# Gates and the next layer's shifts and scales: from two-column matmuls on TensorE to multiply-and-sum over weight rows on VectorE

## The reference: what is computed

```
mod_l = c2 @ w_mod[l] + b_mod[l]              # (2, 3072): shift, scale, gate; 1024 each
h     = x * (1 + scale) + shift
proj  = h @ w_in[l]                           # Hyena, differential attention, MLA, paths, merge gates
...   three branches, each times its SiLU path, through w_branch, gated by sigmoids, summed
out   = merged @ w_out[l]
x     = LayerNorm(alpha * x + gate * out)
```

## Time and profile before

| | us |
|---|---|
| median of 3 runs (2127.22 to 2134.22) | 2133.4 |
| profiled execution, its own time | 2133.02 |
| its span in the trace | 2130.8 |
| PE busy | 1995.7 (94%) |
| DVE busy | 1035.8 (49%) |
| ACT busy | 638.4 (30%) |
| POOL busy | 518.6 (24%) |
| mean granted TensorE clock | 0.966 of full |

### The profile page before, as it was taken

The page is one execution under the profiler, slowest core; times in us unless marked ns, Lnnn a source line. Parts: engine busy times, 40 slices in busy tenths (PEclk is TensorE's granted clock), DMA queues, the critical chain, the costliest instruction groups (busy, mean ns, idle before and its releaser), DMA issues.

```text
span 2130.8 us, 29090 instructions
## 1 busy us (share of the span) xinstructions
PE 1995.7 (94%) x12004; PEld 1722.8 (81%) x12004; DVE 1035.8 (49%) x1486; ACT 638.4 (30%) x1107; POOL 518.6 (24%) x248
## 2 busy tenths in 40 slices
PE   6799989999999999999989999899999999999995
PEld 4578689877886888899886786898778777789995
DVE  3548587355443444322256786845452444442425
ACT  2221322344323343321233122123342344432221
POOL 0211124221231110244222121331222311114640
PEclk9899999999999999999989999999999999999997
DMA  8001012211211211232431110221112111112331
GB/s 325 30 30 40 30 50 80 60 50 40 96 59 50 73 55 58 77 124 85 157 121 40 30 41 30 70 66 54 45 46 105 44 33 41 50 48 99 107 118 50
DMA packets 49818, 149.52 MB, mean 70 GB/s; under 512 B 11030, under 2 KB 12566, under 8 KB 48664
## 3 DMA queue, kind: packets, MB, share of 16 engines
q1 hardware_dynamic: 49688, 147.67, 21.1%
HBM read 141.07 MB, written 6.59 MB: 69 GB/s over the span
## 4 chain that ended last, share of the span: by engine, by line
PE 76%; DVE 13%; ACT 4%; issue 3%; POOL 2%; DMA 1%; SPq 1%; DVEq 0%; ACTq 0%; POOLq 0%
PE PS L691 16%; PE PS L696 16%; PE PS L692 16%; PE PS L727 5%; PE PS L869 3%; PE PS L744 3%; PE PS L715 2%; PE PS L986 2%; PE PS L778 2%; PE PS L765 2%; PE PS L762 2%; PE PS L920 2%; ACT work L1039 1%; DVE work L1670 1%; ACT Wh L1039 1%
## 5 line engine op out<-in xcount | busy, mean ns | idle before, releaser
L1621 POOL TENSOR_TENSOR Wl<-W,Wh 128x1024 fp32r<-128x1024 f32 x196 | 439.4, 2244 | 1406.7 <-ACT Wh L1039 1363.4
L691 PE MATMUL PS<-Hh,Wh 128*128 128x320 f32 x2112 | 638.7, 317 | 15.0 <-ACT work L1163 5.0
L692 PE MATMUL PS<-Hl,Wh 128*128 128x320 f32 x2112 | 626.8, 311 | 0.0
L691 PEld LDWEIGHTS PS<-Hh,Wh 128*128 128x128 f32 x2112 | 401.2, 190 | 41.0 <-issue 25.1
L692 PEld LDWEIGHTS PS<-Hl,Wh 128*128 128x128 f32 x2112 | 401.3, 190 | 2.5 <-issue 1.2
L696 PE MATMUL PS<-Hh,Wl 128*128 128x320 f32 x2112 | 331.4, 309 | 0.9 <-POOL Wl L1621 0.9
L696 PEld LDWEIGHTS PS<-Hh,Wl 128*128 128x128 f32 x2112 | 315.1, 188 | 1.5 <-POOL Wl L1621 1.5
L1039 ACT ACTIVATE work<-PS 128x640 f32<-128x640 f32 (+8 forms) x298 | 176.9, 602 | 355.3 <-PE PS L727 97.8
L1275 DVE TENSOR_REDUCE st<-PS 128x1 f32<-128x640 f32 (+1 forms) x160 | 114.8, 718 | 181.1 <-PE PS L920 91.8
L1039 ACT ACTIVATE Wh<-W 128x1024 fp32r<-128x1024 f32 x196 | 185.8, 950 | 56.2 <-DMA W<-in_w_out 28.3
L1138 ACT ACTIVATE th<-PS 128x640 f32<-128x640 f32 x64 | 45.1, 705 | 343.0 <-PE PS L696 343.0
(11 more groups left out here) (178 smaller groups left out, 2600.4 us busy)
## 6 DMA issues: line engine op xcount, KB each, us to landing
W<-in_w_in SPq DMA_DIRECT2D x132, 512.0 KB, 3.5
W<-in_w_mod SPq DMA_DIRECT2D x32, 512.0 KB, 3.6
W<-in_w_branch SPq DMA_DIRECT2D x48, 256.0 KB, 2.6
pmod_w<-in_w_mod SPq DMA_DIRECT2D x8, 1024.0 KB, 17.4
W<-in_w_out SPq DMA_DIRECT2D x16, 512.0 KB, 3.6
work<-in_x_sample SPq DMA_DIRECT2D x2, 2048.0 KB
x_mid<-work SPq DMA_DIRECT2D x1, 2560.0 KB, 8.5
work<-x_mid SPq DMA_DIRECT2D x1, 2560.0 KB
```

The lines of the kernel that those rows point to most:

```text
L691: pe.matmul(out, Wh[:, b, kk, :], xh[:, kk, t], start=kk == 0, stop=False)
L692: pe.matmul(out, Wh[:, b, kk, :], xl[:, kk, t], start=False, stop=False)
L1621: return pool.tensor_tensor(out, in_, high.bitcast(f32), ALU.subtract)
```

## The change

The 32 blocks are formed without TensorE. The host lays w_mod out by rows: for each block a 128 x 1024 tile whose partition p holds all 1024 weights of output p. Both conditioning rows are put through SiLU as two rows of 1024, stored to memory, and loaded back as `cb`, repeated on all 128 partitions, once per layer (`cload`). A block is then two VectorE `tensor_tensor_reduce` instructions, one per conditioning vector: weights times `cb`, summed over 1024 elements, with the bias as start value and the result in one column of `modc`. A new step `mload` has ScalarE issue the load of a weight tile, and wait first for the VectorE step that last read that buffer. There are three such buffers for the first 17 blocks of layer 0 and one for all others.

The steps leave latent attention and the place after LayerNorm: they now stand among the path tiles, after the merge pairs, and (layer 0 only) behind the wo steps. gmod and nmod no longer take a PSUM slot, nor a place among the `W` tiles. SyncE waits for the 17th block of layer 0 before it loads layer 1's tables. Some tables move to other addresses, and one more constant is loaded at the start.

```
-def weave(a, b): ...
+MOD_PATH, MOD_MERGE, MOD_OUT = ((0, 1, 1, 1), (0, 0, 1, 1)), ((2, 2, 1, 2, 2, 1, 2, 2), (1,) * 6 + (0, 0)), ((1,) * 7 + (0,), (0,) * 8)
+MODS = [[("gmod", g) for g in range(KD)] + [("nmod", g) for g in range(2 * KD if l < DEPTH - 1 else 0)] for l in range(DEPTH)]
+def mod_buffer(l, m):
+    return m % 3 if l == 0 and m < EARLY[0] else 0
+class ModSteps:
+    def loads(self):
+        while self.loaded < len(MODS[self.l]):
+            at, users = mod_user(self.l, self.loaded)
+            if at and users[at - 1][0] == self.l and users[at - 1][1] >= self.done:
+                break
+            steps.append(("mload", self.loaded))
+            self.loaded += 1
+    def take(self, n):
+        for _ in range(n):
+            steps.append(MODS[self.l][self.done])
+            self.done += 1
+            steps += self.loads()
...
-    s += head(0, 2) + head(0, NT - 1) + attention_steps("ml", MH, weave(merge_steps(1), gmods[:KD - 2] + nmods[:NMOD_EARLY - 2]), head)
-    s += path_steps(2) + merge_steps(2) + gmods[KD - 2:] + nmods[NMOD_EARLY - 2:NMOD_EARLY]
+    s += head(0, 2) + head(0, NT - 1) + attention_steps("ml", MH, merge_steps(1), head)
+    for c, step in enumerate(path_steps(2)):
+        s += [step] + ([("cload", 0)] + mods.loads() if c == 0 else []) + mods.take(MOD_PATH[l][c])
+    for d in range(KD):
+        s += merge_steps(2)[2 * d:2 * d + 2] + mods.take(MOD_MERGE[l][d])
     for d in range(KD):
         s += [("wo", d)]
         if d:
             s += [("xt", d - 1)]
+        s += mods.take(MOD_OUT[l][d])
...
-    return s + [("xt", KD - 1), ("ln", 0)] + nmods[NMOD_EARLY:]
+    return s + [("xt", KD - 1), ("ln", 0)]
...
+                        sp.wait_ge(*mod_done(l, EARLY[l] - 1))
                         layer_tables(l + 1)
...
-                    if kind in ("nmod", "gmod"):
-                        ...
-                        for k in range(KD):
-                            last = pe.matmul(ps[:, 0:2], W[:, g % NW, k, :], ccol[:, k, :], ...)
...
+                    if kind == "cload":
+                        act.wait_ge(c_saved, 16)
+                        act.dma_start(cb..., c_silus....partition_broadcast(128)).then_inc(c_here, 16)
+                    elif kind == "mload":
+                        at_, users = mod_user(l, i)
+                        if at_:
+                            act.wait_ge(*mod_done(*users[at_ - 1]))
+                        act.dma_start(modw[mod_buffer(l, i)], A["w_mod_rows"][len(MODS[0]) * l + i])\
+                           .then_inc(mod_here[mod_buffer(l, i)], 16)
...
+                    elif kind in ("gmod", "nmod"):
+                        dve.wait_ge(mod_here[mod_buffer(l, n)], 16 * (mod_user(l, n)[0] + 1))
+                        for j in range(2):
+                            ins = dve.tensor_tensor_reduce(mod_early if n < EARLY[l] else mod_late, modw[mod_buffer(l, n)],
+                                                           cb[:, j], scale, bmods[:, at_, m:m + 1], ALU.mult, ALU.add,
+                                                           modcs[:, at_ % 2, m, j:j + 1])
+                            if j == 0:
+                                link(ins)
+                        ins.then_inc(sems[name], 1)
+                        dve.wait_ge(*mod_done(l, n))
```

More of the change, by code:

```diff
@@ L87, in merge_steps, with mod_user, __init__ @@
     return [(kind, KD * n + d) for d in range(KD) for kind in ("mgate", "mbranch")]
[L90 to L98, removed]
+MOD_PATH, MOD_MERGE, MOD_OUT = ((0, 1, 1, 1), (0, 0, 1, 1)), ((2, 2, 1, 2, 2, 1, 2, 2), (1,) * 6 + (0, 0)), ((1,) * 7 + (0,), (0,) * 8)
+MODS = [[("gmod", g) for g in range(KD)] + [("nmod", g) for g in range(2 * KD if l < DEPTH - 1 else 0)] for l in range(DEPTH)]
+EARLY = [sum(MOD_PATH[l]) + sum(MOD_MERGE[l]) for l in range(DEPTH)]
+assert all(EARLY[l] + sum(MOD_OUT[l]) == len(MODS[l]) for l in range(DEPTH))
+def mod_buffer(l, m):
+    return m % 3 if l == 0 and m < EARLY[0] else 0
+def mod_user(l, m):
+    users = [(a, n) for a in range(DEPTH) for n in range(len(MODS[a])) if mod_buffer(a, n) == mod_buffer(l, m)]
+    return users.index((l, m)), users
+class ModSteps:
+    def __init__(self, l):
+        self.l, self.done, self.loaded = l, 0, 0
+    def loads(self):
+        steps = []
+        while self.loaded < len(MODS[self.l]):
[4 more added lines that the diff above has]
+            self.loaded += 1
+        return steps
+    def take(self, n):
+        steps = []
+        for _ in range(n):
+            steps.append(MODS[self.l][self.done])
+            self.done += 1
+            steps += self.loads()
+        return steps
 def layer_steps(l):
@@ L177 @@
 NP = 5
-SPLIT = [(kind, i) for kind, i in STEPS[0] if owned(kind, i) and kind not in ("nmod", "gmod")]
+SPLIT = [(kind, i) for kind, i in STEPS[0] if owned(kind, i)]
 NSPLIT = len(SPLIT)
@@ L264, in upto_table @@
     for l in range(DEPTH):
-        places = [n for n, step in enumerate(STEPS[l]) if step in SPLIT_AT]
+        steps = [(n, step) for n, step in enumerate(STEPS[l]) if step[0] not in ("gmod", "nmod", "cload", "mload")]
+        places = [n for n, (_, step) in enumerate(steps) if step in SPLIT_AT]
         table[l, STEPS[l].index(("ht", 0))] = 1
         for n, (a, b) in enumerate(zip(places, places[1:])):
-            table[l, a if b - a <= 2 else a + 1] = n + 2
+            table[l, steps[a if b - a <= 2 else a + 1][0]] = n + 2
     return table
@@ L474, in build @@
         rT = raw
+        crow, csg = area(BR, 1024, D)[0:2], th[:].rearrange("p a b -> p (a b)")[0:2, 0:D]
+        cb = area(work, 18432, 2, D)
+        modw = [area(work, off, D) for off in (17408, 5120, 6144)]
+        mod_early, mod_late = raw[:].rearrange("p a b -> p (a b)")[:, 0:D], area(BR, 1024, D)
         PS = [ctx.enter_context(nc.psum_tensor(f"PS{i}", [128, 1024], f32)) for i in range(SLOTS)]
@@ L489, in build @@
         x_saved = sem("x_saved")
+        c_rows = sem("c_rows_ready")
+        c_saved = sem("c_rows_saved")
+        c_here = sem("c_rows_here")
+        mod_here = [sem(f"modulation_weights_here{i}") for i in range(3)]
         consts_here = sem("consts_here")
```

81 lines of the change are left out of this document (44 added, 37 removed).

## The result

The change makes the kernel slower: the median of 9 runs is 2140.74 us (2136.24 to 2145.85), against 2133.4 us for 9 runs of the kernel before on the same chip (2126.89 to 2135.64). The ratio is 1.0042, its 95% interval 1.0027 to 1.0057. The forecast was 2146 us, so the direction was right and the size was 5 us too large. The profiled execution took 2142.03 us with a span of 2139.9 us, against 2133.02 and 2130.8 us: 9.1 us more.

A forecast was written before the change was run, and what follows sets the result against it. TensorE, busy 94% of the span, was taken as the bound on average, with VectorE time free. From 2133.0 us, 27.2 removed and 40.5 added gave 2146.3, so 2146 us; range 2119 to 2172.

The forecast's parts named there:

- The main mechanism: Paths and third merges: ScalarE's wait for VectorE delays Wh copies; 6.7 and 4.0 us at paths, 14.0 and 9.9 at merges.
- rival 4: Loads from ScalarE's queue come late where layer 1 has one buffer, giving about 2155 us; chance 0.04.
- The price of a block: On VectorE: 1.23 us product plus 0.16 us for the sum, 1.39 us an instruction, 2.8 us a block.
- Rival 2: The accumulating VectorE instruction runs at half rate, 5.2 us a block, giving 2210 us; chance 0.10.
- Attention: the step that failed: Latent attention: removing 22 steps at 1.14 us each saves 25.1 us; bounds 38.5 and some 15 us.
- rival 1: Attention gives all 38.5 us back and waits at the blocks are short, 31 us added, giving 2124 us; chance 0.29.
- rival 3: Ten pauses of 2 to 3 us lower TensorE's clock, 2.1 us each, giving 2166 us; chance 0.10.
- The four steps behind layer 0's third merge: Their removal gains nothing by itself, since tile wo 2's late load, behind layer 1's tables, sets the end.
- wo 2 and the low clock behind its pause: Layer 0's output projection: wo 2 starts 2.0 us later and low clock loses 2.1 us, together 4.1 us.
- The delay of wo 6 behind its block: Layer 0's output projection: two more blocks on VectorE put the copy of wo 6 1.4 us later (0 to 3).
- Layer 1 starts 2.1 us sooner behind the norm: After layer 0's LayerNorm: removing four modulation steps that end 2.1 us after VectorE finishes the norm gains 2.1 us.
- The start: One more constant in SyncE's queue ahead of all loads adds 0.45 us.

The follow-up runs named there:

- experiment 1: Changed kernel with each mload among path and third-merge tiles placed behind the next path or mgate tile's copy: 2112.09 us, ratio 0.9904.
- experiment 5: Changed kernel with mloads in the third merge placed behind the next mbranch tile, among paths behind the next path tile: 2101.19 us, ratio 0.9863.
- experiment 2: Changed kernel with each sum over only the first 512 of 1024 products, steps and loads unmoved: 2109.44 us, ratio 0.9892.
- experiment 8: Kernel before the change, with layer 1's merge tiles in attention at layer 0's places, its six modulation steps kept: 2129.95 us, ratio 0.9994.
- experiment 3: Changed kernel with layer 1's merge tiles in attention at their old uneven places, no modulation steps between: 2152.11 us, ratio 1.0095.
- experiment 7: Kernel before the change, with tile wo 2 loaded ahead of layer 1's tables: 2130.18 us, ratio 0.9999.
- experiment 9: Changed kernel with mloads behind the next mbranch tile, plus layer 0's wo 2 and wo 3 loaded ahead of layer 1's tables: 2095.97 us, ratio 0.9831.
- experiment 6: Changed kernel with later mloads, wo 2 loaded ahead of the tables, and two blocks behind each of layer 0's first seven pairs: 2103.39 us, ratio 0.9872.
- experiment 4: Changed kernel with layer 0's tile wo 2 loaded before the wait for block 17 and layer 1's tables: 2131.82 us, ratio 1.0004.

## Why the prediction was right, and where it was wrong

The main mechanism held, in its place and its size: ScalarE's wait for VectorE, taken for the load, delays a copy that TensorE needs. Forecast and measured pauses (us):

| place | forecast | measured |
|---|---|---|
| paths, layer 0 | 1.9, 2.6, 2.2 | 1.69, 1.97, 1.61 |
| paths, layer 1 | 4.0 for two | 1.69, 1.60 |
| double blocks, layer 0 | 3.2, four times | 3.13, 3.13, 3.13, 3.15 |
| lone blocks, layer 0 | 0.4, three times | 0.47, 0.49, 0.47 |
| merge, layer 1 | 0.4 three times, 2.9 three times | 0.47, 1.82, 0.47, 2.84, 2.85, none |

Together 34.6 us forecast, 19.2 + 11.7 = 30.9 measured. The paths cost less than I had (5.3 and 3.3 us for 6.7 and 4.0), and two more places differ. The last block of layer 1 lets no load go, so it holds nothing up; I had counted it. And the 1.82 is rival 4, at one place: the block itself waited for its tile.

```profile
1976.22 1.28 DVE L1374 CUSTOM_DVE_ANT_0 raw<-work,b_mod 128x1024 f32<-128x1024 f32 x1 [2.78 <-DMA work<-in_w_mod_rows]
```

Taking the wait out of the copy's way (experiments 1 and 5) and shortening it (2) both gave most of that back. So this is shown, not argued.

**The price of a block.** Estimated 1.39 us an instruction. All 64 of the trace:

```profile
L1374 DVE DVE_READ_ACCUMULATOR2_ANT modc<- x64: 76/82/85, 888.6 to 2033.5; 128x1 f32 x64
L1374 DVE CUSTOM_DVE_ANT_0 raw<-work,b_mod x50: 1283/1285/2699, 885.9 to 2032.3; 128x1024 f32<-128x1024 f32 x50
L1374 DVE CUSTOM_DVE_ANT_0 BR<-work,b_mod x14: 1283/1285/3294, 1018.9 to 1093.4; 128x1024 f32<-128x1024 f32 x14
```

(minimum, median, maximum in ns, then the first and last start). 1.285 + 0.08 = 1.37 us. The page of the Trainium skill that the prediction weighed, "Vector Engine (DVE) Microarchitecture Reference", section "Points that are easy to get wrong", would have it at half throughput; the measurement decides against it, since a plain product of the same size takes 1.23 us. Rival 2 is out.

**Attention: the step that failed.** I read 1.14 us a step off two layers that differ by ten steps, and gave all 22 that price: -25.1 us. Measured: -25.3 and -12.3, so -37.6 in all, close to my upper bound of 38.5 and to rival 1's first half. Busy time fell by 28.0 us for 16 steps (1.75 each, as counted) and by 11.2 for 6 (1.9 each). The error was in the waits: I took it that TensorE stands still the more, the fewer steps are left, so that 0.61 us of each step's 1.75 comes back. Of 39.2 us of busy time 1.6 came back. TensorE stands still for 4.8 us with 16 steps, for 8.6 with 6 steps or 10.6 with 6 at even places (experiment 8), and for only 7.8 us with none, but for 13.8 with none at the old places (experiment 3). A straight line through two points, between which the places of the merge tiles had changed too, said nothing of the third. Why waits shrink from 6 steps to none at even places is open.

The other half of what I missed is the clock. With the steps in attention its granted clock is below full: 0.98 in layer 0 in all three traces of that order (before, experiments 7 and 8), and 0.97, 0.97 and 0.99 in layer 1. With the steps gone it is 1.00 or 0.99 in layer 0 in all eight traces, and so it is in layer 1 but for experiment 3 (0.98). So part of the 1.75 us is most likely not the step's own work but a lower clock over it and the matmuls around it. The same stretch of layer 0 in experiments 5 and 9, without and with 3.4 us at 1.2 GHz, gives a price:

```profile
658.00:868.50 210.50, 202.67 (x1194) 161.96 (x1192) 96.12 (x176) 89.64 (x182) 29.14 (x16) 1.00 0.11 34
```

```profile
652.90:864.80 211.90, 204.12 (x1194) 162.57 (x1192) 96.08 (x176) 89.61 (x182) 29.14 (x16) 0.99 0.10 34
```

That is 1.4 us. An estimate from it: in the two attention stages TensorE was at 1.2 GHz for 10.2 and 13.7 us before, and for 0 and 3.4 us after, so 20.5 us less, some 8 of the 37.6 us. I had left this term at nothing.

**The clock in paths and merge: left at nothing too.** That is rival 3 in part. The same matmuls were busy 8.4 us longer in layer 0 and 3.4 us longer in layer 1, 11.8 us over 17 pauses (the rival had 20 for ten). Three windows of the kernel after:

```profile
925.00:940.00 15.00, 12.24 (x69) 11.97 (x67) 8.71 (x11) 0.47 (x2) 3.93 (x2) 0.84 0.35 111
940.00:955.00 15.00, 14.16 (x85) 13.89 (x86) 6.13 (x7) 4.03 (x6) 6.91 (x5) 0.89 0.40 123
955.00:985.00 30.00, 23.72 (x150) 23.20 (x149) 17.45 (x22) 4.34 (x6) 11.04 (x7) 0.94 0.38 125
```

Behind the pause that ends at 940.37 TensorE is at 1.2 GHz up to 943.4 and does 11 matmuls in 3.3 us; from 943.5 on it is at 2.4 GHz and does 75 in 11.5 us:

```profile
940.10:943.40 3.30, 3.03 (x11) 3.03 (x12) 0.00 (x0) 1.76 (x3) 2.75 (x2) 0.50 0.68 191
943.50:955.00 11.50, 11.03 (x75) 10.76 (x75) 6.13 (x7) 2.17 (x3) 4.06 (x4) 1.00 0.32 103
```

With layer 0's pauses down to 1.7 us and less (experiment 1) its clock is 1.00, and it is 1.00 with sums of half length (experiment 2) too. So in layer 0 it is shown that the clock is lost with the long pauses and comes back without them. In layer 1 it is less clear: 0.99 in the changed kernel with pauses of up to 2.85 us, 0.96 with nearly the same pauses in experiment 3, still 0.99 in experiments 1 and 2 with pauses of up to 2.07 and 1.78 us, and 1.00 only in experiments 5, 6 and 9, where one pause of 0.73 us is left. The stretches at 1.2 GHz don't answer to the pauses one to one, and what a single pause costs isn't shown.

**The steps without a change.** The four steps behind layer 0's third merge I held to be worth nothing, since a transfer sets wo 2: right, wo 2 starts 32.1 us behind the merge, where I had about 33. The two-column steps were shadowed by that load, and experiments 4 and 7 show the load as the bound and 6.7 us as their price without it. For wo 2 and the low clock behind its pause I had 4.1 us: wo 2 is 1.5 us later, and wo 3 follows it at 9.8 us where it was 7.6, 3.7 together. The delay of wo 6 behind its block was 1.3 us (10.7 against 9.4), forecast 1.4. Layer 1 starts 2.1 us sooner behind the norm, as said: its first tile comes 30.6 us behind wo 7 instead of 32.7.

The start is 3.4 us longer, where I had 0.45. Nearly all of that is chance. In the kernel after, TensorE is at 1.2 GHz from 414.4 to 417.8 and from 585.0 to 588.4 us, ahead of anything that the change touches; in the kernel before it isn't. But experiment 7, of the order of before, has the same two, and experiment 2, of the order of after, has neither. The first of them in the kernels before and after and in experiments 7 and 2, in this order:

```profile
414.40:417.80 3.40, 3.40 (x25) 3.40 (x24) 1.50 (x3) 1.17 (x3) 1.49 (x1) 1.00 0.00 0
```

```profile
414.40:417.80 3.40, 3.40 (x15) 3.40 (x14) 2.03 (x5) 1.76 (x5) 1.47 (x1) 0.50 0.00 0
```

```profile
414.40:417.80 3.40, 3.40 (x15) 3.40 (x14) 2.04 (x5) 1.78 (x5) 1.46 (x1) 0.51 0.00 0
```

```profile
414.40:417.80 3.40, 3.40 (x25) 3.40 (x25) 1.79 (x5) 1.52 (x5) 1.49 (x1) 1.00 0.00 0
```

Latent attention of layer 0 starts at 654.5, 657.9, 658.0 and 654.8 us in them. So some 3 us of the start are not the change's. As much goes the other way: from its first tile to latent attention layer 1 takes 587.4 us in the kernel before and 584.4 after, work that the change doesn't touch, and it took 584.0 to 589.1 us in the experiments. The two cancel in the 9.1 us between the profiled executions; the medians differ by 7.3.

**The sum again**, by the measured terms: -37.6 (attention) -2.1 (behind the norm) + 30.9 (pauses) + 11.8 (clock in paths and merge) + 1.5 (to wo 2) + 2.2 (wo 3) + 1.3 (wo 6) + 3.4 (start, mostly chance) - 3.0 (layer 1 ahead of attention, chance) + 0.7 (behind the last merge) = +9.1, as in the profile. That the forecast of +13 came out near is luck: two errors cancelled, since attention gave 12.5 us more and the clock in paths and merge took 11.8 us.

## What to carry to other kernels

A transfer's issue that waits for one engine must not stand ahead of another engine's urgent work in the same queue: here 39.5 us (2140.7 against 2101.2) lay in the place of that one step, and none of it needed a faster engine. With that wait gone the next bound shows: two blocks behind every pair fill VectorE, and the last pairs take 11.9 us instead of 10.6 (experiment 6). When work is moved from a full engine to an idle one, list what is queued behind each new wait, not just the busy time it adds. And don't read the price of a step off two stages that differ in more than the number of steps.

## What the runs showed of the hardware

- A fused multiply-and-sum on VectorE shows as two instructions, 1285 ns for 128x1024 and 82 ns to read the sum; 750 ns for 128x512. That is 1.04 ns a column from one to the other.
- Beside GpSimd's MGl such a sum takes 2.69 us, and up to 3.29 us beside a GpSimd instruction of 128x1024, so 1.4 to 2.0 us longer than alone. In the kernel after 21 of the 64 sums took over 1.3 us, and each of them overlaps a GpSimd instruction. MGl itself takes 1.57 us there. A sum of half the length grows by as much, from 0.75 to 2.15 us.
- In layer 0's merge and behind it TensorE of the kernel after was at 1.2 GHz from 923.0, 940.0, 967.3 and 1011.7 us, for 3.4 or 6.8 us each time. Each time began within a pause of 3 to 4 us or up to 0.4 us behind its end; a pause of 3.15 us that ended at 982.5 had none.
- It comes by chance as well: the stretches at 414.4 and 585.0 us are in some executions and not in others with the same work there, whichever the kernel, and moved the start of attention by 3 us.
- Where the two-column matmuls with 128x128 weights stand, the clock is lower: 0.98 in layer 0's attention with 16 such steps and 1.00 or 0.99 without, and four steps in a row had 0.60.
